# Gates of the first token tile: one-hot products on TensorE, or adding scatters issued from GpSimd

## The chip, the cores and the metric

The kernel runs on one core of one Trainium2 chip. TensorE multiplies, VectorE (DVE), ScalarE (ACT) and GpSimd (POOL) work on tiles in on-chip memory, SyncE (SP) issues most DMAs, and 16 DMA engines move the data. Every engine works through a queue of its own in order, and the queues wait for each other by semaphores. The metric is the device time in microseconds of one execution, as the median of several runs; a profile is one further execution of its own.

## The reference, cut to what matters

Two transformer blocks run over 512 tokens of width 1024. The first (convolution and sliding attention, then a feed forward of width 2816) and the attention of the second are not touched, apart from DMAs set beside the feed forward. The change is in the last layer of the second block, which picks 128 of 16384 experts for every token, 16 in each of 8 heads:

```python
def peer(xn, wq, subkeys, u_tab, v_tab):
    q = (xn @ wq).reshape(bsz, s, PEER_HEADS, 2, PEER_HALF)
    sub = jnp.einsum('bshpd,hpnd->bshpn', q, subkeys, preferred_element_type=jnp.float32)
    s_top, i_top = lax.top_k(sub, PEER_TOPK)
    cand = (s_top[..., 0, :, None] + s_top[..., 1, None, :]).reshape(...)
    cand_idx = (i_top[..., 0, :, None] * N_KEYS + i_top[..., 1, None, :]).reshape(...)
    best, pos = lax.top_k(cand, PEER_TOPK)
    expert = jnp.take_along_axis(cand_idx, pos, axis=-1)
    gate = jax.nn.softmax(best, axis=-1)
    ...
        a = jax.nn.gelu(jnp.einsum('td,ted->te', xb, ub, preferred_element_type=jnp.float32))
        return jnp.einsum('te,ted->td', (gb * a).astype(vb.dtype), vb)
```

## The kernel before

The 512 tokens are four tiles of 128. Three of them (TD = 384 tokens) go **dense**: all 16384 experts are computed for them, 128 at a time (a "unit" x of 128 experts, NEXP = 128 units), and weighted by a gate matrix that is zero where an expert was not chosen. The fourth tile goes **by rows**: GpSimd gathers the chosen rows of the two tables, 128 rows each, one table row for each token per gather.

Dense, up: for unit x TensorE makes a 128 x 384 product in 24 matmuls (8 chunks, each in three products of high and low parts: L449, L452, L453). ScalarE applies the gelu (L1538) and SP stores it to DRAM (`activations`, L1027).

Dense, gates: for each token the gate matrix is a 128 x 128 matrix, the sum over its 128 choices of a one-hot column times a one-hot row times the gate. VectorE makes the one-hots of four tokens (a "four") in two instructions (L2268, L2272, tile `hots`), TensorE multiplies them (four matmuls, L930; the trace has two records for each), ScalarE copies the result into `Gs` (L1567). After 16 fours (64 tokens) ScalarE issues a 4 MB DMA of `Gs` into the DRAM tensor `gate_matrices` (gd, L1572). It holds TSTAY = 256 tokens; the last 128 of the 384 stay in `Gs`. `fours_of(x)` says which fours follow the product of unit x: the 96 fours lie behind the 64 units from FIRST_GATE_UP = 43 on, one and two in turn. The lists of choices are turned by TensorE first (L922, tile `sel`).

Dense, down: for each unit VectorE multiplies activation and gate (`weigh`, L2301, L2302) and TensorE adds 18 products into six banks. SP fetches activation and gate rows back (`load_weighing`, L1035, L1036), the first NAG = 4 units together at unit LOAD_AT = 124 of the up stage.

Rows: GpSimd issues 256 gathers (L1118, rows of `y`, four buffers, so gather r waits until row r - 4 is used). VectorE uses each: for the first 128 a row product (L2247), for the others a multiply-add into hN (L2255). `rows_until` sets how many rows stand in VectorE's queue before each unit: one per unit in the 64 units with gates, eight in five units after them.

Weights: unit by unit through three buffers `wraw`; SP loads (L987), ScalarE rounds to the high part `WH` (L1139), VectorE subtracts to get the low part `WL` (L2236; GpSimd does so before the expert stage, L1110). What sets the order is the order of the written loops on each engine. In the up stage VectorE's loop is, for unit x: one-hots of unit x + 1, the rows of unit x, `WL` of unit x + 2.

## Time and profile before

| | |
|---|---|
| median of 3 runs | 2197.84 us (2195.1 to 2200.02) |
| the profiled execution | 2191.74 us, of it a span of 2190.0 us |
| TensorE busy | 2142.9 us, 98% of the span |
| VectorE, ScalarE, GpSimd busy | 1477.7, 886.4 and 856.1 us |
| feed forward, weights issued | 214 to 572 us |
| up stage with gates | first hots product 1218.8 us, last 1566.6 us |

The span is what lies between the first and the last instruction; the profile's times are counted from its start. "Busy" is the time under instructions. The idle time before an instruction is given with the event that ended it. A wait of an engine matters if the engine that ends last stands behind it.

### The profile page before, as it was taken

The page shows a single profiled execution, that of the slowest core. Times are in us where ns is not written, and L with a number is a line of the kernel's source. Part 1 is how long each engine was busy: PE and PEld are TensorE (multiplying, and loading weights), DVE is VectorE, ACT ScalarE, POOL GpSimd, SP SyncE. Part 2 cuts the span into 40 slices and gives each one's busy share as a digit, 9 for nine tenths or more (in the row PEclk, how much of TensorE's full clock was granted, in tenths as well). Part 3 has the DMA queues.
Part 4 walks back from the last instruction along what each step waited for, and adds up shares of the span by engine and source line. Part 5 has one row for each costly group of instructions (what it writes and reads, how often), then busy time and mean ns, then how long its engine had stood idle before and what let it go on. Part 6 is the DMA issues. An engine that isn't in the chain of part 4 may idle for free.

```text
span 2190.0 us, 29584 instructions
## 1 busy us (share of the span) xinstructions
PE 2142.9 (98%) x10879; PEld 1864.9 (85%) x10879; DVE 1477.7 (67%) x2763; ACT 886.4 (40%) x1341; POOL 856.1 (39%) x450
## 2 busy tenths in 40 slices
PE   7989999999999999999999999999998999999999
PEld 6757888888877877899999999999997888888887
DVE  5973411110146994346879999999767999999887
ACT  5355422232253444343334555555433333333332
POOL 1003244444333433345667422222343455434452
PEclk9999999999999999999999999999999999999999
DMA  5302233333342322344444899997799999999996
GB/s 176 97 7 65 93 97 97 97 98 87 92 121 68 88 67 86 97 138 135 132 136 147 269 307 295 302 290 260 255 358 333 374 372 380 376 374 365 375 351 256
DMA packets 222219, 444.10 MB, mean 203 GB/s; under 512 B 83803, under 2 KB 133884, under 8 KB 221948
## 3 DMA queue, kind: packets, MB, share of 16 engines
q1 hardware_dynamic: 119612, 291.20, 39.5%
q0 software_dynamic: 36864, 134.23, 17.2%
q10 hardware_dynamic: 65600, 16.78, 3.4%
q8 instruction: 87, 1.43, 0.3%
q14 instruction: 56, 0.46, 0.1%
HBM read 397.71 MB, written 44.43 MB: 202 GB/s over the span
## 4 chain that ended last, share of the span: by engine, by line
PE 87%; DVE 7%; ACT 2%; DMA 2%; issue 1%; POOL 1%; SPq 0%; DVEq 0%; ACTq 0%; POOLq 0%
PE bank L449 26%; PE bank L452 26%; PE bank L453 26%; PE bank L930 4%; DVE cacc L1734 1%; DMA wraw<-in_peer_u 1%; DVE m L1927 1%; PE bank L899 1%; POOL WL L1110 1%; DVE xn L1928 1%; PE bank L621 1%; ACT sc L1250 1%; ACT WH L1139 0%; PE bank L836 0%; DMA wraw<-in_w_in 0%
## 5 line engine op out<-in xcount | busy, mean ns | idle before, releaser
L1110 POOL TENSOR_TENSOR WL<-wraw,WH 128x1024 fp32r<-128x1024 f32 x182 | 467.7, 2575 | 736.7 <-ACT WH L1139 736.7
L1139 ACT ACTIVATE WH<-wraw 128x1024 fp32r<-128x1024 f32 x411 | 435.2, 1060 | 619.1 <-PE bank L449 341.0
L449 PE MATMUL bank<-XH,WH 128*128 128x384 f32 (+2 forms) x1864 | 668.4, 359 | 12.3 <-DVE WL L2236 5.2
L452 PE MATMUL bank<-XL,WH 128*128 128x384 f32 (+2 forms) x1864 | 657.9, 353 | 0.0
L453 PE MATMUL bank<-XH,WL 128*128 128x384 f32 (+2 forms) x1864 | 657.9, 353 | 0.0
L449 PEld LDWEIGHTS bank<-XH,WH 128*128 128x128 f32 x1864 | 352.0, 189 | 44.2 <-issue 11.2
L452 PEld LDWEIGHTS bank<-XL,WH 128*128 128x128 f32 x1864 | 352.0, 189 | 28.5 <-issue 0.7
L453 PEld LDWEIGHTS bank<-XH,WL 128*128 128x128 f32 x1864 | 351.4, 189 | 28.5
L2236 DVE TENSOR_TENSOR WL<-wraw,WH 128x1024 fp32r<-128x1024 f32 x229 | 279.6, 1222 | 105.5 <-ACT WH L1139 98.9
L1118 POOL DMA_INDIRECT y<-in_peer_u_rows,gidx x128 | 182.1, 1423 | 356.8 <-DVE gdot L2247 346.3
L449 PE MATMUL bank<-WH,GH 128*128 128x512 f32 x768 | 299.2, 390 | 1.9 <-issue 1.6
L453 PE MATMUL bank<-WH,GL 128*128 128x512 f32 x768 | 298.9, 389 | 0.0
L452 PE MATMUL bank<-WL,GH 128*128 128x512 f32 x768 | 298.8, 389 | 0.0
L1118 POOL DMA_INDIRECT y<-in_peer_v,gidx x128 | 204.2, 1595 | 209.2 <-DVE hN L2255 188.1
L449 PEld LDWEIGHTS bank<-WH,GH 128*128 128x128 f32 x768 | 144.2, 188 | 33.4 <-issue 3.5
L453 PEld LDWEIGHTS bank<-WH,GL 128*128 128x128 f32 x768 | 144.2, 188 | 29.9
L452 PEld LDWEIGHTS bank<-WL,GH 128*128 128x128 f32 x768 | 144.2, 188 | 29.7
L2255 DVE SCALAR_TENSOR_TENSOR hN<-y,gdot,hN 128x1024 f32<-128x1024 f32 x128 | 163.7, 1279 | 2.9
L1538 ACT ACTIVATE ac<-bank 128x384 f32<-128x384 f32 x122 | 59.7, 490 | 241.7 <-PE bank L453 237.3
L1852 DVE TENSOR_TENSOR y<-bank,y 128x512 f32<-128x512 f32 x22 | 15.2, 691 | 208.2 <-PE bank L453 208.2
L2247 DVE CUSTOM_DVE_ANT_0 y<-y,x_nat 128x1024 f32<-128x1024 f32 x128 | 154.8, 1219 | 1.2 <-DMA y<-in_peer_u_rows,gidx 1.1
L2268 DVE TENSOR_TENSOR hots<-iota,sq 128x1024 f32<-128x1024 f32 x96 | 117.1, 1219 | 2.7 <-ACT rt L1549 2.7
(304 smaller groups left out, 2577.9 us busy)
## 6 DMA issues: line engine op xcount, KB each, us to landing
wraw<-in_peer_u SPq DMA_DIRECT2D x128, 512.0 KB
wraw<-in_peer_v SPq DMA_DIRECT2D x128, 512.0 KB
activations<-ac SPq DMA_DIRECT2D x122, 192.0 KB
ar<-activations SPq DMA_DIRECT2D x122, 192.0 KB
gate_matrices<-Gs ACTq DMA_DIRECT2D x4, 4096.0 KB, 35.7
gr<-gate_matrices SPq DMA_DIRECT2D x128, 128.0 KB
wraw<-in_w_gate SPq DMA_DIRECT2D x22, 512.0 KB
wraw<-in_w_up SPq DMA_DIRECT2D x22, 512.0 KB
```

The costliest lines, as they stand in the source:

```text
L449: mm = pe.matmul(out, wh, xh, start=first, stop=False)
L452: pe.matmul(out, wh, xl, start=False, stop=False)
L453: return pe.matmul(out, wl, xh, start=False, stop=last)
L930: mm = pe.matmul(out[:, r * P:(r + 1) * P], hots[:, q, 1, r, :], hots[:, q, 0, r, :], start=True, stop=True)
L1110: pool.tensor_tensor(WL[:, u % NW, 0:m], wraw[:, u % NR, 0:m], WH[:, u % NW, 0:m].bitcast(F32), ALU.subtract).then_inc(s("w_lo"), 1)
L1118: pool.indirect_dma_start(out=gathered[:, row % NGATHER, :], out_offset=None, in_=(u_rows if row < HS else v_rows)[:, :], in_offset=bass.I ...
L1139: act.activation(WH[:, u % NW, 0:k * n], wraw[:, u % NR, 0:k * n], ACT.Copy).then_inc(s("w_hi"), 1)
L1538: act.activation(ac[:, x % NAC, :] if x < SENT else kept[:, x - SENT, :], src[:, 0:TD], ACT.Gelu_apprx_tanh).then_inc(frees(("a", x)), 1)
L2236: dve.tensor_tensor(WL[:, u % NW, 0:k * n], wraw[:, u % NR, 0:k * n], WH[:, u % NW, 0:k * n].bitcast(F32), ALU.subtract).then_inc(made, 1)
L2247: dve.tensor_tensor_reduce(out=at, in0=at, in1=x_nat[:, :], scale=1.0, scalar=0.0, op0=ALU.mult, op1=ALU.add, accum_out=gdot[:, row:row + ...
L2255: dve.scalar_tensor_tensor(out=hN[:, NTD, :], in0=at, scalar=gdot[:, row - HS:row - HS + 1], in1=hN[:, NTD, :], op0=ALU.mult, op1=ALU.add) ...
L2268: link(dve.tensor_tensor(hots[:, q, :, :, :], iota128[:, :].unsqueeze(1).unsqueeze(1).to_broadcast([P, 2, TOK4, P]), ijcol[:, :, tok].unsq ...
```

## The change

The first of the three dense tiles no longer has its gates formed by TensorE. `fours_of` now deals out 64 fours over the same 64 units, one each, and the sel tile of the first token tile isn't turned. In place of that:

- SP writes zeros over the first tile's part of `gate_matrices`, in 16 DMAs of 512 KB (runs of 256 B), one after every fourth weight load from feed forward unit ("wg", 4) on.
- VectorE makes, behind `gidx`, the addresses of the first tile's gates: (expert number) x 256 + token (three instructions: `scat_expert`, `scat_gate`, `scat_at`).
- GpSimd issues 128 indirect DMAs that add: number k adds, for each of the 128 tokens, its gate k to its cell in DRAM. Two follow each of the first 64 gathers. Before every sixteenth it waits until all earlier ones have landed, since two heads may have chosen the same expert.
- Of the 4 MB stores of `Gs` the first two fall away.
- SP loads the first gates and activations back from unit 120 on, one pair every second unit, and waits at unit 120 for all scatters.

```diff
...
+TSCAT = P
+FIRST_FOUR = TSCAT // TOK4
...
+SCAT_PER_ROW = 2
+ZRUN = 64
+ZBLOCKS = 8
-LOAD_AT = NEXP - 4
+LOAD_AT = NEXP - 2 * NAG
...
-    return range(b * NFOUR // GATE_UPS, (b + 1) * NFOUR // GATE_UPS)
+    fours = NFOUR - FIRST_FOUR
+    return range(FIRST_FOUR + b * fours // GATE_UPS, FIRST_FOUR + (b + 1) * fours // GATE_UPS)
...
+        with ExitStack() as under:
+            scat_at = sb("scat_at", [P, HS], U32, under)
+            scat_gate = sb("scat_gate", [P, HS], F32, under)
+            scat_expert = sb("scat_expert", [P, HS], F32, under)
...
+        own_row = sb("own_row", [P, 1], F32)
...
+            zeros = sb("zeros", [P, ZRUN], F32, sc)
...
+        gate_cells = gd.rearrange("x p (t a) -> (x p t) a", a=1)
...
                     if x == FIRST_GATE_UP - UP_AFTER_SEL:
-                        for t in range(NTD):
+                        for t in range(TSCAT // P, NTD):
...
                     tile(("u", x), ("a", x), tokens=TD)
                     for four in fours_of(x):
                         out = take("gm", four)
-                        pe.wait_ge(s("hots_made"), four + 1)
+                        pe.wait_ge(s("hots_made"), four - FIRST_FOUR + 1)
                         q = four % NQ
...
+                if u >= unit_at[("wg", 4)] and (u - unit_at[("wg", 4)]) % 4 == 0 and u < unit_at[("wg", 4)] + 4 * (NEXP // ZBLOCKS):
+                    if u == unit_at[("wg", 4)]:
+                        sp.wait_ge(s("zeros_made"), 1)
+                    half, x = (u - unit_at[("wg", 4)]) // 4 % 2, (u - unit_at[("wg", 4)]) // 8 * 2 * ZBLOCKS
+                    sp.dma_start(gd[x:x + 2 * ZBLOCKS, :, half * ZRUN:(half + 1) * ZRUN].rearrange("x p t -> p x t"),
+                                 zeros[:, :].unsqueeze(1).to_broadcast([P, 2 * ZBLOCKS, ZRUN])).then_inc(
+                                     s("zeroed"), 16)
...
                         if x == LOAD_AT:
                                 wait_full(sp, ("gm", four))
-                            for tt in range(NGT - NGSTAY):
+                            sp.wait_ge(s("scattered"), 16 * HS)
+                            for tt in range(TSCAT // GTOK, NGT - NGSTAY):
                                 sp.wait_ge(s(f"g_out{tt}"), 16)
-                            for n in range(NAG):
-                                load_weighing(n)
+                        if x >= LOAD_AT and (x - LOAD_AT) % 2 == 0:
+                            load_weighing((x - LOAD_AT) // 2)
...
+            pool.iota(own_row[:, :], pattern=[[1, 1]], base=0, channel_multiplier=1,
+                      allow_small_or_imprecise_dtypes=True).then_inc(s("own_row_made"), 1)
+            pool.memset(zeros[:, :], 0.0).then_inc(s("zeros_made"), 1)
...
+            def scatter(k):
+
+                if k == 0:
+                    pool.wait_ge(s("scatter_made"), 1)
+                    pool.wait_ge(s("zeroed"), 16 * (NEXP // ZBLOCKS))
+                elif k % SEL == 0:
+                    pool.wait_ge(s("scattered"), 16 * k)
+                pool.indirect_dma_start(out=gate_cells[:, :],
+                                        out_offset=bass.IndirectOffsetOnAxis(ap=scat_at[:, k:k + 1], axis=0),
+                                        in_=scat_gate[:, k:k + 1], in_offset=None, compute_op=ALU.add).then_inc(
+                                            s("scattered"), 16)
+
             for row in range(2 * HS):
...
                                         in_offset=bass.IndirectOffsetOnAxis(ap=gidx[:, row % HS:row % HS + 1], axis=0)
+                for k in range(min(row * SCAT_PER_ROW, HS), min((row + 1) * SCAT_PER_ROW, HS)):
+                    scatter(k)
...
                     if x == FIRST_GATE_UP - UP_AFTER_SEL:
-                        for t in range(NTD):
+                        for t in range(TSCAT // P, NTD):
...
             def copy_gates(four):
                 tt, at = four // per, four % per * TOK4
-                if at == 0 and tt >= 2:
+                if at == 0 and tt >= TSCAT // GTOK + 2:
...
+                expert = step(dve.scalar_tensor_tensor(out=scat_expert[:, :], in0=sel[:, 0, 0, :], scalar=float(N_KEYS),
+                                                       in1=sel[:, 1, 0, :], op0=ALU.mult, op1=ALU.add))
+                dve.tensor_copy(scat_gate[:, :], sel[:, 2, 0, :])
+                dve.wait_ge(s("own_row_made"), 1)
+                dve.wait_ge(s("dve_link"), expert)
+                dve.scalar_tensor_tensor(out=scat_at[:, :], in0=scat_expert[:, :], scalar=float(TSTAY),
+                                         in1=own_row[:, 0:1].to_broadcast([P, HS]), op0=ALU.mult, op1=ALU.add).then_inc(
+                                             s("scatter_made"), 1)
...
                     for four in fours_of(x):
-                        if four >= NQ:
+                        if four >= FIRST_FOUR + NQ:
...
-                for t in range(NTD):
+                for t in range(TSCAT // P, NTD):
```

GpSimd's queue, from the end of the weight work on. Before:

```order
L1110 TENSOR_TENSOR WL<-wraw,WH 128x1024 [waits w_begun,w_hi] x100
L1118 DMA y<-in_peer_u_rows,gidx 128x1024 [waits index_made]
```

After (scat_gate holds the gates, scat_at the addresses):

```order
L1134 TENSOR_TENSOR WL<-wraw,WH 128x1024 [waits w_begun,w_hi] x100
L1154 DMA y<-in_peer_u_rows,gidx 128x1024 [waits index_made]
L1145 DMA gate_matrices<-scat_gate,scat_at 4194304x1 [waits zeroed,scatter_made]
L1145 DMA gate_matrices<-scat_gate,scat_at 4194304x1
L1154 DMA y<-in_peer_u_rows,gidx 128x1024
L1145 DMA gate_matrices<-scat_gate,scat_at 4194304x1 x2
```

Gathers 1, 2 and 3, which followed each other directly, now stand behind two, four and six scatters.

VectorE's queue at the beginning of the stage, from the end of the choice of experts. Before:

```order
L2225 SCALAR_TENSOR_TENSOR gidx<-sel 128x128
L2228 COPY ggate<-sel 128x128
L2236 TENSOR_TENSOR WL<-wraw,WH 128x1024
L2268 TENSOR_TENSOR hots<-iota,sq 128x1024
L2272 TENSOR_TENSOR hots<-hots,rt 128x512
L2236 TENSOR_TENSOR WL<-wraw,WH 128x1024
L2247 ISA y,gdot<-y,x_nat 128x1024
L2247 ISA gdot 128x1
L2247 ISA y,gdot<-y,x_nat 128x1024
L2247 ISA gdot 128x1
L2268 TENSOR_TENSOR hots<-iota,sq 128x1024
L2272 TENSOR_TENSOR hots<-hots,rt 128x512
```

After:

```order
L2263 SCALAR_TENSOR_TENSOR gidx<-sel 128x128
L2266 COPY ggate<-sel 128x128
L2267 SCALAR_TENSOR_TENSOR scat_expert<-sel 128x128
L2269 COPY scat_gate<-sel 128x128
L2272 SCALAR_TENSOR_TENSOR scat_at<-scat_expert,own_row 128x128
L2282 TENSOR_TENSOR WL<-wraw,WH 128x1024
L2314 TENSOR_TENSOR hots<-iota,sq 128x1024
L2318 TENSOR_TENSOR hots<-hots,rt 128x512
L2282 TENSOR_TENSOR WL<-wraw,WH 128x1024
L2293 ISA y,gdot<-y,x_nat 128x1024
```

Three instructions are added ahead of the WL of the next unit; where two pairs of hots stood (every second unit), one pair stands.

SP's queue where the first gates are loaded back. Before:

```order
L1027 DMA activations<-ac 128x384
L1035 DMA ar<-activations 128x384
L1036 DMA gr<-gate_matrices 128x256
L1035 DMA ar<-activations 128x384
L1036 DMA gr<-gate_matrices 128x256
L1035 DMA ar<-activations 128x384
L1036 DMA gr<-gate_matrices 128x256
L1035 DMA ar<-activations 128x384
L1036 DMA gr<-gate_matrices 128x256
L987 DMA wraw<-in_peer_u 128x1024 x3
```

After:

```order
L1040 DMA activations<-ac 128x384
L1048 DMA ar<-activations 128x384
L1049 DMA gr<-gate_matrices 128x256
L1000 DMA wraw<-in_peer_u 128x1024
L1040 DMA activations<-ac 128x384
L1000 DMA wraw<-in_peer_u 128x1024
L1040 DMA activations<-ac 128x384
L1048 DMA ar<-activations 128x384
L1049 DMA gr<-gate_matrices 128x256
L1000 DMA wraw<-in_peer_u 128x1024
```

Eight loads that stood together are four pairs, with two weight loads between one pair and the next.

## Rows read from the trace of the kernel before

**Rows 1.** The page: span, busy times, the DMA engines in 40 slices (tenths busy).

```profile
span 2190.0 us, 29584 instructions
...
PE 2142.9 (98%) x10879; PEld 1864.9 (85%) x10879; DVE 1477.7 (67%) x2763; ACT 886.4 (40%) x1341; POOL 856.1 (39%) x450
...
DMA  5302233333342322344444899997799999999996
```

**Rows 2.** Waits of TensorE, whole span: us in total, times, longest.

```profile
PE bank L498 <- DVE y L1635: 11.6, 3, 9.0
...
PE bank L449 <- DVE WL L2236: 5.2, 1, 5.2
```

**Rows 3.** Windows: length, busy us (count) by engine, clock, DMA share, GB/s.

```profile
1205.00:1310.00 105.00, 105.00 (x682) 104.97 (x682) 98.34 (x118) 55.27 (x73) 37.74 (x24) 1.00 0.88 285
1310.00:1415.00 105.00, 105.00 (x690) 105.00 (x690) 98.03 (x118) 58.46 (x68) 26.60 (x19) 1.00 0.93 295
1415.00:1570.00 155.00, 155.00 (x1016) 155.00 (x1015) 137.67 (x166) 82.59 (x98) 40.60 (x29) 1.00 0.84 269
1570.00:1660.00 90.00, 84.84 (x479) 84.33 (x478) 60.95 (x85) 29.57 (x40) 45.32 (x32) 0.96 0.94 337
```

**Rows 4.** Timeline of TensorE: start, duration, count; transposes of sel, then gate products.

```profile
1209.51 1.14 PE L922 MATMUL bank<-ident,sel 128*128 128x128 f32 x9
...
1542.89 1.95 PE L930 MATMUL bank<-hots 128*128 128x128 f32 x16
1544.60 0.42 PE L449 MATMUL bank<-XH,WH 128*128 128x384 f32 x1
...
1548.84 1.05 PE L930 MATMUL bank<-hots 128*128 128x128 f32 x8
1549.65 0.42 PE L449 MATMUL bank<-XH,WH 128*128 128x384 f32 x1
```

**Rows 5.** A group of 1205 to 1570 us: count, busy us, mean ns, idle before, releasers.

```profile
L1118 POOL DMA_INDIRECT y<-in_peer_u_rows,gidx x71 | 102.4, 1442 | 256.5 <-DVE gdot L2247 255.0 <-issue 0.9 <-DVE gidx L2225 0.7
```

**Rows 6.** Timeline of POOL: start, duration, in brackets the idle time before.

```profile
1210.44 0.94 POOL L1118 DMA_INDIRECT y<-in_peer_u_rows,gidx  x1 [0.31 <-issue]
...
1212.93 0.97 POOL L1118 DMA_INDIRECT y<-in_peer_u_rows,gidx  x1 [0.30 <-issue]
...
1300.68 1.68 POOL L1118 DMA_INDIRECT y<-in_peer_u_rows,gidx  x1 [2.46 <-DVE gdot L2247]
```

**Rows 7.** Timeline of VectorE at the same places.

```profile
1207.61 0.29 DVE L2225 SCALAR_TENSOR_TENSOR gidx<-sel 128x128 uint32<-128x128 f32 x1
1207.96 1.22 DVE L2236 TENSOR_TENSOR WL<-wraw,WH 128x1024 fp32r<-128x1024 f32 x1
1211.86 1.23 DVE L2268 TENSOR_TENSOR hots<-iota,sq 128x1024 f32<-128x1024 f32 x1 [2.68 <-ACT rt L1549]
1216.89 1.23 DVE L2247 CUSTOM_DVE_ANT_0 y<-y,x_nat 128x1024 f32<-128x1024 f32 x1 [0.81 <-DMA y<-in_peer_u_rows,gidx]
...
1300.33 1.22 DVE L2236 TENSOR_TENSOR WL<-wraw,WH 128x1024 fp32r<-128x1024 f32 x1
1301.46 1.22 DVE L2268 TENSOR_TENSOR hots<-iota,sq 128x1024 f32<-128x1024 f32 x1
1302.72 0.69 DVE L2272 TENSOR_TENSOR hots<-hots,rt 128x512 f32<-128x512 f32 x1
```

**Rows 8.** DMA queues: packets, MB, share of 16 engines' span.

```profile
q0 software_dynamic: 36864, 134.23, 17.2%
q10 hardware_dynamic: 65600, 16.78, 3.4%
```

**Rows 9.** Around the eight loads: SP, ScalarE, TensorE in time.

```profile
1632.30 0.30 SPq L1035 DMA_DIRECT2D ar<-activations  x1
...
1644.63 1.06 ACT L1139 ACTIVATE WH<-wraw 128x1024 fp32r<-128x1024 f32 x1 [8.33 <-DMA wraw<-in_peer_u]
...
1647.09 0.66 PE L449 MATMUL bank<-XH,WH 128*128 128x384 f32 x1 [5.16 <-DVE WL L2236]
```

## The prediction

> **What bounds the kernel now.** The page first: TensorE is busy 98% of a 2190.0 us span, and the granted clock is full in the stretches that matter here, 1.00 [rows 1, 3]. The waits of TensorE, whole span: one of 9.0 us, one of 5.2 us [rows 2], and none of the others above 3.4. So time comes off only if TensorE gets less work or loses a wait, and comes on as soon as another engine's queue falls behind. The windows over the stretch in which the gates are made then show how near the others are [rows 3]: VectorE is busy 98 of 105 us, the DMA engines 0.88 and 0.93, POOL (GpSimd) 38 and 27 of 105. From 1570 to 1660 us the DMA share is 0.94 and TensorE is short by 5.2 us. The change acts on this stretch.
>
> **Part 1, TensorE's gate products (removed: a third).** After each expert's 24 products come one or two "fours". In the timeline a unit followed by two fours has its 16 records from 1542.89 and goes on at 1544.60, 1.71 us; with one four from 1548.84 to 1549.65, 0.81 us [rows 4]. Before: 96 fours in 64 units, so 32 units with two and 32 with one: 32 x 1.71 + 32 x 0.81 = 80.6 us. After: 64 fours, one per unit: 64 x 0.81 = 51.8 us. Gain 28.8 us, all on the path, since TensorE waited for nothing there. Three of the nine transposes of sel go too, nine took 1.14 us [rows 4]: 0.4 us. A whole unit with one four runs from 1544.60 to 1549.65, 5.05 us; one with two is 0.90 longer, so the mean was 5.50 and the 64 units take 323 instead of 352 us.
>
> **Part 2, VectorE and ScalarE.** Each dropped four takes 1.22 + 0.69 us from VectorE [rows 7] and one copy from ScalarE, which is busy half of the stretch [rows 3]. VectorE per unit: one four 1.91, one row product 1.23, one WL 1.22 = 4.36 of 5.05 us [rows 7], 86% where the windows have 89 to 94% [rows 3]. It gains air. Three small instructions are added behind gidx, at about 0.3 us each (gidx took 0.29 [rows 7]), 0.8 us before the WL that the next unit needs; that WL started at 1207.96 us [rows 7] and its unit at 1214.6 (the first hots product starts at 1218.8 us, less one expert product of 1544.60 to 1548.84 = 4.2 us [rows 4]), so they cost nothing.
>
> **Part 3, POOL: the term that decides.** POOL issued one gather per unit and gets two scatters to each of the first 64. No scatter is in this trace; the nearest row is the gather's issue, also DMA_INDIRECT with 128 indices. Its time is not constant. With VectorE idle at its start it takes 0.94 us, and issues follow each other at 0.30 us of "issue" [rows 6]: 1.25 us each. The one at 1300.68 took 1.68: it began while VectorE ran WL from 1300.33 to 1301.55, and 1300.68 + 1.68 = 1302.36 is 0.81 after that instruction's end, though VectorE went straight on with another [rows 6, 7]. The one at 1212.93 began under the first hots instruction (1211.86 to 1213.09) and ended 0.81 after its end as well [rows 6, 7]. So an issue waits for the VectorE instruction that is running at its start, then needs 0.81 us of its own; the next starts 0.81 + 0.30 = 1.11 us behind a VectorE boundary, just as an instruction of 1.22 us ends that began at the boundary (WL at 1300.33, the next at 1301.46: 1.13 us apart [rows 7]). If the scatter costs what the gather does, POOL gets one issue per long VectorE instruction, and the 0.69 us one lets it slip: three issues per unit. Three are wanted. The Trainium skill has this as a rule ("SBUF — State Buffer", section "Who interferes with whom": a VectorE instruction with two SBUF inputs and a GpSimd one that reads SBUF exclude each other for the whole instruction); the trace agrees, by the 0.81 us.
> The same from the sums: from 1205 to 1570 us POOL's 71 issues took 102.4 us at 1.44 mean, and it was idle 256.5 us [rows 5]. 64 rows' share of that is 231 us, less the 29 us saved: 202 us. 128 scatters need 128 x 1.25 = 160 us at best, 128 x (1.44 + 0.30) = 223 at the mean, 128 x 1.98 = 254 if each met a running instruction. I take the low end, since back-to-back issues start near a boundary.
> Queued behind POOL: the gathers, and behind those VectorE's row product, which stands ahead of WL in VectorE's order, and behind WL TensorE. The cover is the lead of four rows: a gather may go out 4 units (20 us) ahead and lands about 6.4 us after its issue (second gather at 1210.44, VectorE waited for it until 1216.89 [rows 6, 7]), so 13 us of lateness are hidden. At the start there is no lead: gather 1 now goes out after two scatters, near 1213, and VectorE waits some 2.5 us longer; TensorE sees about 1 us, as the WL behind the next row product is wanted two units after 1214.6, at 1224.7. Every 16 scatters POOL waits until all earlier ones have landed. They lie in one queue behind a gather with 6.4 us to land: 2 to 3 us, 7 times, 14 to 21 us against the 13 us of cover: 1 to 8 us, I take 2. Part 3 in all: +3 us, bounds +1 and +9 while the scatter's issue costs the gather's.
>
> **Part 4, DMA.** 16.78 MB of gate stores took 3.4% of 16 engines' span, 74 us, for 65600 packets of 256 B: 18 ns each [rows 8]. Half goes: -37 us of DMA time in the stretch. The zeroing is the same 37 us (32768 packets), but beside the feed forward, which runs from 214 to about 580 us, slices 5 to 11, 0.2 to 0.4 busy [rows 1]: 16 DMAs of 2.3 us each, a weight load then lands at most 2.3 us later and is prefetched three units ahead; nothing. The scatters add 128 x 128 = 16384 element packets; at 18 ns 18 us, at a 4 KB packet's time (17.2% of 16 x 2190 us over 36864 packets = 163 ns [rows 8]) 167 us. I take the low end, for the size. DMA time of the stretch was 0.88 x 105 + 0.93 x 105 + 0.84 x 155 = 320 us of 365 [rows 3]; it becomes 320 - 37 + 18 = 301 of 336: 0.90, as before, no cost.
>
> **Part 5, the loads of gates and activations, spread.** SP issued eight loads in a row from 1632.30 us, 1.25 MB, ahead of a weight load. ScalarE then waited 8.33 us for that weight load and TensorE 5.16 us [rows 9]; the granted clock of the window is 0.96 [rows 3]. 21 units lie between the last hots product (1566.6 + 0.8) and the first product of the down stage (1663.1, behind 1.6 us of issue), 94 us; at 0.173 us a product they need 21 x 4.16 = 87.4: 6.6 us lost. Now a pair of loads goes out every second unit from unit 120. SP waits there for the scatters too, but their last is issued near unit 105. The bytes stay, at a share of 0.94, so not all comes back: -4 us, bounds 0 and -6.6.
>
> **Sum.** -28.8 - 0.4 + 3 + 0 - 4 = -30 us. The profiled run has 2191.7 us (span 2190.0), the median of the runs 2197.8, 6 us above. Forecast on the median: 2168 us. Its own bounds: -29.2 + 1 - 6.6 = -35, and -29.2 + 9 + 0 = -20, with some more if the clock dips: 2160 to 2185.
>
> **Rivals.**
> A, slower: POOL becomes the pace. If the scatter's own time is not 0.81 but 1.2 to 1.6 us (one and a half times to twice the gather's, which no row excludes), the next issue comes 1.5 to 1.9 us behind a VectorE boundary, in the middle of the second instruction, and waits for that one's end near 2.3. A scatter then costs two VectorE instructions, a unit 2 x 2.3 + 1.1 = 5.7 us at least, 6.0 with the waits for landings. 64 units: 365 to 384 us against 352 before: +13 to +32, less 4 of part 5: 2207 to 2226 us, and up to 2240 if the landings add more. It decides from about 0.2 us more per scatter. For it: the 202 us of room against 223 at the mean. Against: same instruction, same 128 indices. The Trainium skill ("Collectives: The Full Stack", section "Stop ④ — SDMA + CCE: where bytes move and the add happens") describes an add in the DMA engine as two reads and one write; no row here shows an adding DMA, and by that rule alone this rival would be the forecast if POOL's 0.81 us went mostly into read descriptors.
> B, no change, or a small gain: scatters a little dearer (0.1 to 0.2 us), POOL falls behind in some units; units of 5.2 to 5.5 us. 64 x 0.15 to 0.45 = 10 to 29 us given back, more with the waits: 2185 to 2206 us.
> C, the element packets are slow. 16384 at 52 ns (53 us) fill the 336 us; at 80 ns the stretch is as long as before; at 163 ns it needs 283 + 167 = 450 us, +85: up to 2280 us. Long landings would do the same through the seven waits. The stretch is already near 0.9, which speaks for it.
> D, the change does less than it says: POOL ends its scatters later than unit 120 and SP blocks the weights. It would take a pace of 6 us or more, and belongs to A and C.
>
> **How the numbers follow.** Forecast 45%. B 14%, A 26%, C (and worse) 15%. Range for 8 in 10: 2160 to 2245, leaving out 3% below and most of C above. About 0.2% (4.4 us) is what a measurement of this kernel can tell from no change: faster by more than that holds the forecast and half of B: 52%. Within it: 6%. Slower: the rest of B, A, C: 42%.
>
> **What would show it.** Part 1: 512 records of hots products instead of 768, a unit of 5.05 us. Part 3 right: scatter issues of 0.94 to 1.7 us, VectorE's waits for gathered rows small, TensorE's waits for WL small between 1215 and 1540 us. Wrong (A): scatter issues above 1.2 us with VectorE idle, POOL busy or at "issue" without a break over the first 64 rows, VectorE waiting for y at most rows, TensorE for WL. C: DMA share at 1.0, POOL waiting for its own scatters, ScalarE for wraw. Part 4: TensorE's waits in the feed forward unchanged. Part 5: the 5.16 us wait gone, clock 1.0 there. The forecast fails as a whole if the gathers land late.

## Result and profile after

The changed kernel takes 2239.82 us (median of 6 runs, 2233.04 to 2240.76) against 2198.93 us for the kernel before on the same chip (6 runs): a ratio of 1.0188, 95% interval 1.0173 to 1.0202. It is **slower by 41 us**, where the forecast was 30 us faster. The profiled execution has a span of 2239.2 us, 49.2 more than before's.

Where the 49 us lie, by the landmarks of the two traces:

| | before | after | difference |
|---|---|---|---|
| first hots product starts | 1218.8 | 1226.6 | +7.8 |
| first to last hots product | 347.8 | 386.5 | **+38.7** |
| last hots product to first product of the down stage | 96.5 | 96.7 | +0.2 |
| down stage and end | 526.9 | 529.4 | +2.5 |

So nearly all of it is in the stretch from the first to the last hots product, called the stage below, where TensorE has a third less of gate products to do. Lines of the page that answer to [rows 1] (busy us, share of the span, instructions; then the DMA engines in 40 slices):

```profile
span 2239.2 us, 29066 instructions
...
PE 2144.1 (96%) x10620; PEld 1854.1 (83%) x10620; DVE 1427.0 (64%) x2702; ACT 857.6 (38%) x1306; POOL 1111.2 (50%) x580
...
DMA  4302344444332223344445788977899999999996
```

TensorE is busy as long as before with 259 instructions fewer, VectorE is busy 51 us less, and GpSimd 255 us more. The windows of the stage of after (as in [rows 3]):

```profile
1205.00:1310.00 105.00, 91.35 (x526) 89.90 (x525) 74.44 (x86) 41.17 (x55) 83.44 (x49) 0.93 0.71 195
1310.00:1415.00 105.00, 91.78 (x552) 90.33 (x552) 71.81 (x86) 43.75 (x52) 88.10 (x52) 0.97 0.90 246
1415.00:1570.00 155.00, 137.35 (x805) 135.90 (x805) 106.03 (x126) 62.64 (x75) 131.33 (x78) 0.93 0.86 230
```

In the first two windows GpSimd (the fifth busy figure of a line) went from 38 and 27 to 83 and 88 of 105 us, VectorE fell from 98 to 74 and 72, and TensorE from 105 to 91 and 92. The clock fell from 1.00 to 0.93 to 0.97. The DMA share went from 0.88, 0.93 and 0.84 to 0.71, 0.90 and 0.86, while the bytes moved fell from 285, 295 and 269 to 195, 246 and 230 GB/s. GpSimd's two groups of DMA issues in the up stage (count, busy us, mean ns, idle time before them by what ended it); [rows 5] has the gathers of before:

```profile
L1145 POOL DMA_INDIRECT gate_matrices<-scat_gate,scat_at x128 | 240.6, 1879 | 40.9 <-issue 37.7 <-DMA gate_matrices<-scat_gate,scat_at 3.3
L1154 POOL DMA_INDIRECT y<-in_peer_u_rows,gidx x128 | 178.2, 1392 | 123.5 <-DVE gdot L2293 92.6 <-issue 24.1 <-DVE gidx L2263 6.8
```

Who waits for whom follows from VectorE's and TensorE's waits over the whole span (us in total, times, longest); before, TensorE had one wait for `WL` [rows 2] and VectorE's waits for gathered rows came to 1.1 us:

```profile
DVE y L2293 <- DMA y<-in_peer_u_rows,gidx: 125.9, 61, 6.6
```

```profile
PE bank L462 <- DVE WL L2282: 50.5, 34, 5.2
```

An ordinary row of the stage, first as the chain of what ended last between 1397 and 1412 us (start, us, what):

```profile
1397.07 1.55 POOL gate_matrices L1145
1398.62 0.30 issue
1398.93 1.15 POOL y L1154
1400.07 0.30 issue
1400.38 2.55 POOL gate_matrices L1145
1402.92 0.30 issue
1403.23 1.55 POOL gate_matrices L1145
1404.78 0.30 issue
1405.09 1.07 POOL y L1154
```

and VectorE's timeline in the same row (start, duration, in brackets the idle time before):

```profile
1400.25 1.22 DVE L2314 TENSOR_TENSOR hots<-iota,sq 128x1024 f32<-128x1024 f32 x1
1401.50 0.69 DVE L2318 TENSOR_TENSOR hots<-hots,rt 128x512 f32<-128x512 f32 x1
1404.06 1.23 DVE L2293 CUSTOM_DVE_ANT_0 y<-y,x_nat 128x1024 f32<-128x1024 f32 x1 [1.86 <-DMA y<-in_peer_u_rows,gidx]
```

GpSimd goes through gather, scatter, scatter without a break but the 0.30 us of issue: from 1398.93 to 1405.09, 6.16 us a row. A unit of TensorE with one four needs 5.05. The scatter at 1403.23 began with VectorE idle and took 1.55 us. The one at 1400.38 began under the hots instruction that ended at 1401.47 and itself ended 1.46 us after that. It is the pattern that the prediction read from the gathers, with 1.46 us where it put 0.81. GpSimd's first gather began at 1216.49 and its 65th at 1606.52: 64 rows in 390 us, 6.09 us a row. The stage, which is 63 units and a little more, has 386.5 us, 6.12 us a unit.

### The profile page after: what moved, and what is told of

The parts are those of the page before. It is cut to its first block, busy times and chain, and to the rows that moved or that the text cites. A ratio compares the mean times of both kernels' runs of the same rounds, so it can differ in the third digit from the quotient of the medians.

```text
span 2239.2 us, 29066 instructions
## 1 busy us (share of the span) xinstructions
PE 2144.1 (96%) x10620; PEld 1854.1 (83%) x10620; DVE 1427.0 (64%) x2702; ACT 857.6 (38%) x1306; POOL 1111.2 (50%) x580
## 3 DMA queue, kind: packets, MB, share of 16 engines
q0 software_dynamic: 55296, 134.31, 18.9%
## 4 chain that ended last, share of the span: by engine, by line
PE 68%; POOL 13%; DVE 6%; DMA 6%; issue 4%; ACT 2%; SPq 0%; DVEq 0%; ACTq 0%; POOLq 0%
PE bank L462 21%; PE bank L465 21%; PE bank L466 21%; POOL gate_matrices L1145 9%; POOL y L1154 3%; DMA wraw<-in_peer_u 2%; DMA y<-in_peer_u_rows,gidx 2%; DVE m L1965 1%; DMA wraw<-in_peer_v 1%; PE bank L912 1%; DVE xn L1966 1%; PE bank L634 1%; DMA gate_matrices<-scat_gate,scat_at 0%; ACT WH L1177 0%; PE bank L511 0%
## 5 line engine op out<-in xcount | busy, mean ns | idle before, releaser
L1134 POOL TENSOR_TENSOR WL<-wraw,WH 128x1024 fp32r<-128x1024 f32 x182 | 476.7, 2625 | 729.7 <-ACT WH L1177 729.7
L462 PE MATMUL bank<-XH,WH 128*128 128x384 f32 (+2 forms) x1864 | 676.5, 363 | 56.7 <-DVE WL L2282 50.5
L466 PE MATMUL bank<-XH,WL 128*128 128x384 f32 (+2 forms) x1864 | 664.8, 357 | 0.0
L462 PEld LDWEIGHTS bank<-XH,WH 128*128 128x128 f32 x1864 | 357.4, 192 | 95.1 <-issue 62.6
L465 PEld LDWEIGHTS bank<-XL,WH 128*128 128x128 f32 x1864 | 357.8, 192 | 28.6 <-issue 0.7
L466 PEld LDWEIGHTS bank<-XH,WL 128*128 128x128 f32 x1864 | 356.5, 191 | 28.6
L1154 POOL DMA_INDIRECT y<-in_peer_v,gidx x128 | 213.4, 1667 | 201.3 <-DVE hN L2301 177.0
L1145 POOL DMA_INDIRECT gate_matrices<-scat_gate,scat_at x128 | 240.6, 1879 | 40.9 <-issue 37.7
```

The lines of the kernel that those rows point to most:

```text
L462: mm = pe.matmul(out, wh, xh, start=first, stop=False)
L465: pe.matmul(out, wh, xl, start=False, stop=False)
L466: return pe.matmul(out, wl, xh, start=False, stop=last)
L1134: pool.tensor_tensor(WL[:, u % NW, 0:m], wraw[:, u % NR, 0:m], WH[:, u % NW, 0:m].bitcast(F32), ALU.subtract).then_inc(s("w_lo"), 1)
L1145: pool.indirect_dma_start(out=gate_cells[:, :], out_offset=bass.IndirectOffsetOnAxis(ap=scat_at[:, k:k + 1], axis=0), in_=scat_gate[:, k:k ...
L1154: pool.indirect_dma_start(out=gathered[:, row % NGATHER, :], out_offset=None, in_=(u_rows if row < HS else v_rows)[:, :], in_offset=bass.I ...
```

## The experiments

The question is what makes GpSimd's row so long, and whether it alone costs the time. **Theory A**: the issue of an accumulating scatter (one that adds) is dearer than a gather's, GpSimd becomes the pace of a row, VectorE waits for gathered rows and TensorE for VectorE. Against it stand rival C (the element packets, or their landings), a price for each scatter wherever it stands, and a share for the zeroing and the later start.

**One scatter in place of 128** (all else as changed; in each run with fewer scatters the number that SP waits for at unit 120 follows, which the diffs don't show):

```diff
-                for k in range(min(row * SCAT_PER_ROW, HS), min((row + 1) * SCAT_PER_ROW, HS)):
+                for k in range(row, row + 1) if row < 1 else ():
```

> The changed kernel with one scatter instead of 128: the gates of the first token tile are then left out of the matrix, apart from one pick's. Zeroing, TensorE's two tiles, the spread loads and all 256 gathers stay. Theory A (GpSimd's issue of the scatters, 240.6 us of its time, is what VectorE and then TensorE wait for): VectorE's waits for gathered rows fall from 125.9 us to under 10, TensorE's 34 waits of 50.5 us for the hot rows go, its clock stays whole in the stage, and the stage of the gate products comes to about 318 us (347.8 less the 28.8 of half the products, and little more); the whole at 2165 to 2180 us. Rival C (the accumulating packets hold the DMA queues up) expects the same time here, so this run alone doesn't part the two; its DMA waits would say so. Rival: the later start (the transposes 6.4 us later) and the zeroing cost something of their own, then it stays at 2185 or above.

Measured: 2166.74 us, ratio 0.9861 (0.9837 to 0.9885). First to last hots product: 1222.8 to 1542.3 us, 319.5 us. The window over that stretch:

```profile
1222.60:1542.40 319.80, 319.80 (x2028) 319.80 (x2026) 266.12 (x320) 159.12 (x190) 72.04 (x66) 1.00 0.86 281
```

TensorE is busy in all of it, at full clock. Without its scatters the change thus comes out where it was forecast (2168 us), and the 73 us between this run and the change come with the other 127 scatters. VectorE's instructions aren't slowed by them: some 320 took 266 us here and 317 took 265 in the change (the line stands under **The clock** below). VectorE waits.

**64 scatters, one a row:**

```diff
-                for k in range(min(row * SCAT_PER_ROW, HS), min((row + 1) * SCAT_PER_ROW, HS)):
+                for k in range(row, row + 1) if row < HS // 2 else ():
```

> The changed kernel with 64 scatters instead of 128, one beside each of the first 64 gathers; the other half of the first tile's gates is left out. Theory A: GpSimd has in each of these rows one gather of 1.39 and one scatter of 1.88 us, 3.3 us in place of 6.1, against a row of VectorE and TensorE of about 4.5 us (318 us over some 71 rows), so it is not the pace of the row any more; the stage stays near 325 us and the whole at 2170 to 2190 us, nearly all of the loss gone with half the scatters. A cost that were in proportion to the scatters (each at its own price on the path, or each packet's in the DMA queues) would leave half of the loss: about halfway between the run with one scatter and the change, 2200 to 2210 us.

Measured: 2171.81 us, ratio 0.9883 (0.9862 to 0.9905). The stage is 319.6 us, as with one scatter, though each scatter takes GpSimd as long as in the change:

```profile
L1145 POOL DMA_INDIRECT gate_matrices<-scat_gate,scat_at x64 | 120.4, 1882 | 25.4 <-issue 18.9 <-DMA gate_matrices<-scat_gate,scat_at 6.5
```

Half of the scatters cost 5 us of the 73. The two profiles are 7.6 us apart, and 5.3 of these are there already at `gidx` (1217.4 and 1212.1), ahead of the first scatter. A cost in proportion is out.

**96 scatters**, one and two a row by turns (`range(row * 3 // 2, (row + 1) * 3 // 2)` over 64 rows in place of the same loop):

> The changed kernel with 96 accumulating scatters, one and two by turns beside each of the first 64 gathers; a quarter of the first tile's gates is left out. The runs so far: one scatter 2166.7 us, 64 scatters 2171.8, 128 scatters 2239.8. Theory A with a point from which GpSimd decides: the stage of 319.5 us without loss has 64 rows, 4.99 us a row; with 1.5 scatters a row GpSimd needs about 1.39 + 1.5 x 1.88 + 2.5 x 0.3 = 4.96 us, just at the row, and VectorE is up to four rows behind before it waits. So little is lost: 2172 to 2190 us. If each scatter beyond the 64th costs its share, it is the middle, 2206 us; if the loss is the number of GpSimd's issues in a row of two (a burst that closes the buffer of four rows), nearly half of it as well.

Measured: 2184.08 us, ratio 0.9942 (0.9924 to 0.9960). The curve over 1, 64, 96 and 128 scatters is 2166.7, 2171.8, 2184.1, 2239.8 us: flat, a bend, then 1.7 us for each scatter.

**64 scatters crowded into 32 rows**, the same number at twice the rate:

```diff
-                for k in range(min(row * SCAT_PER_ROW, HS), min((row + 1) * SCAT_PER_ROW, HS)):
+                for k in range(2 * row, 2 * row + 2) if row < HS // 4 else ():
```

> The changed kernel with 64 accumulating scatters, as in the run that took 2171.8 us, but two beside each of the first 32 gathers in place of one beside each of the first 64; half of the first tile's gates is left out. Theory A, the pace of a row: in 32 rows GpSimd needs 6.1 us a row against TensorE's and VectorE's 4.99, 32 x 1.1 = 35 us less the four rows of the buffer (some 6 us), and half-clock stretches of some 5 to 10 us beside it; then it keeps pace. 2197 to 2212 us. Rival, the number of accumulating scatters (their packets, or GpSimd's time beside VectorE, wherever they stand): 2172 us again, within 3.

Measured: 2205.69 us, ratio 1.0032 (1.0020 to 1.0045): 34 us above the run with the same number of scatters one a row. It is their rate that costs, not their number. Two windows (columns as in [rows 3]), the first over the crowded rows:

```profile
1229.00:1410.00 181.00, 159.80 (x955) 157.86 (x954) 125.02 (x150) 75.57 (x90) 151.18 (x91) 0.95 0.86 232
1410.00:1586.00 176.00, 172.80 (x1077) 172.64 (x1076) 143.91 (x173) 82.81 (x100) 42.71 (x40) 0.98 0.87 275
```

TensorE is short by 21 us where GpSimd is busy 151 of 181 us, and by 3 us where it is not.

**Plain writes in place of adding ones**, all 128 at the same places:

```diff
-                                        in_=scat_gate[:, k:k + 1], in_offset=None, compute_op=ALU.add).then_inc(
+                                        in_=scat_gate[:, k:k + 1], in_offset=None).then_inc(
```

> The changed kernel with the accumulation taken out of the scatters: each is a plain write of its 128 gates, same addresses, same 128 issues; where two picks of a token fall on one expert the later one stands alone. Theory A with the cost in the issue of any scattered store: GpSimd's 1.55 us unblocked and 1.88 us mean stay, and the time stays within 3 us of 2240. Rival: the accumulation is what makes the issue longer than the gather's (1.55 against 0.94 us unblocked): then an issue falls to about 0.94, the row of GpSimd to some 4.5 us, and the time to 2190 to 2215 us. By rival C the packets' time falls (no read of the old value), and with it the time, while the issue does not.

Measured: 2193.23 us, ratio 0.9975 (0.9960 to 0.9990). The scatter's line (ns, shortest, median, longest) and its group:

```profile
L1145 POOL DMA_INDIRECT gate_matrices<-scat_gate,scat_at x128: 972/1308/2002, 1217.7 to 1557.9; - x128
```

```profile
L1145 POOL DMA_INDIRECT gate_matrices<-scat_gate,scat_at x128 | 184.1, 1438 | 53.1 <-issue 36.9 <-DMA gate_matrices<-scat_gate,scat_at 16.2
```

With VectorE idle a plain one takes 0.97 us, the adding one 1.55, the gather 0.94. So asking for the add puts 0.58 us on GpSimd's issue, and without it 46.6 us of the loss are gone. The rival that the run was made for holds, and theory A in its narrow form (any scattered store is that dear) does not. The edit changes the packets too: the software queue of this run has 40960, that of the change 55296 and that of before 36864 [rows 8]. The next run halves the packets at the same number of issues.

**Scatters of 64 partitions**, still 128 of them: half of the addresses and packets.

```diff
-                                        out_offset=bass.IndirectOffsetOnAxis(ap=scat_at[:, k:k + 1], axis=0),
-                                        in_=scat_gate[:, k:k + 1], in_offset=None, compute_op=ALU.add).then_inc(
+                                        out_offset=bass.IndirectOffsetOnAxis(ap=scat_at[0:P // 2, k:k + 1], axis=0),
+                                        in_=scat_gate[0:P // 2, k:k + 1], in_offset=None, compute_op=ALU.add).then_inc(
```

> The changed kernel with all 128 accumulating scatters, but each of 64 partitions in place of 128: half the packets and half the addresses at the same number of issues; the gates of tokens 64 to 127 are left out. If an issue costs by its count of addresses, unblocked it falls from 1.55 to about 0.8 to 1.0 us, GpSimd's row from 6.1 to about 4.9 us, and the time to 2175 to 2200 us. If it costs a fixed amount for each issue, it stays at 1.55 and the time at 2235 to 2245 us, although the DMA queues have half the scatter packets: that would also close the case against the packets (rival C).

Measured: 2232.49 us, ratio 1.0153 (1.0132 to 1.0175), 7 us below the change, and a little below the range that was expected of a fixed price.

```profile
L1145 POOL DMA_INDIRECT gate_matrices<-scat_gate,scat_at x128: 1417/1500/2469, 1218.3 to 1595.2; - x128
```

Half the addresses take 0.14 us off an issue of 1.55: most of it is a fixed price. And half of the scatters' addresses and packets took 7 us off, no more than the shorter issues explain (128 x 0.09 us of mean, 11.7 us). Rival C is closed for this kernel: had the packets been the bound, about half of the 73 us would have gone.

**Part 4 alone**, the zeroing DMAs in the kernel before:

```diff
+                if u >= unit_at[("wg", 4)] and (u - unit_at[("wg", 4)]) % 4 == 0 and u < unit_at[("wg", 4)] + 4 * (NEXP // ZBLOCKS):
...
+                    sp.dma_start(gd[x:x + 2 * ZBLOCKS, :, half * ZRUN:(half + 1) * ZRUN].rearrange("x p t -> p x t"),
+                                 zeros[:, :].unsqueeze(1).to_broadcast([P, 2 * ZBLOCKS, ZRUN])).then_inc(
+                                     s("zeroed"), 16)
```

> The kernel before with part 4 alone: the sixteen zeroing DMAs beside the feed forward, the rest as before. The change's gate stage began 7.8 us later than before's, the one-scatter run's 3.8, the others' 5 to 9. If the zeroing did it: 2200 to 2205 us, with the first peer_u weights landing some 3 us later. If that start only drifts from run to run (the one-scatter and 64-scatter programs are the same up to there and differ by 5 us): within 1.5 us of 2196.7.

Measured: 2195.48 us, ratio 0.9993 (0.9983 to 1.0002). The zeroing costs nothing that can be told from noise. The first hots product starts at 1222.7 us, 3.9 later than in the profile of before. The next run has no zeroing and starts it at 1221.9, so the zeroing isn't what moves this start.

**Part 5 alone**, the spread loads in the kernel before:

```diff
-LOAD_AT = NEXP - 4
+LOAD_AT = NEXP - 2 * NAG
...
-                            for n in range(NAG):
-                                load_weighing(n)
+                        if x >= LOAD_AT and (x - LOAD_AT) % 2 == 0:
+                            load_weighing((x - LOAD_AT) // 2)
```

> The kernel before with part 5 of the change alone: the waits for the written gates and the first pair of loads stand at the first of the last eight gate units, and a pair of loads follows at every second unit, in place of all eight together four units before the end. The prediction gave it 4 us (0 to 6.6): 2191 to 2198 us. The change's own trace showed 96.7 us from the last hot product to the first down product against 96.5 before: by that it is worth nothing there, within 1 us of 2197.8; and where the loads wait for the fourth tile half's gates earlier, SP could hold back weight loads: up to 2205 us.

Measured: 2193.82 us, ratio 0.9987 (0.9975 to 0.9999), 2.9 us faster, which is only just clear of nothing. TensorE's waits from 1570 to 1665 us:

```profile
PE bank L449 <- DVE WL L2236: 2.2, 1, 2.2
PE bank L449 <- issue: 1.6, 1, 1.6
```

The wait of 5.16 us [rows 9] is 2.2, and from the last hots product to the down stage it is 93.5 us instead of 96.5.

**A version of what was learned: 64 tokens scattered, one scatter a row.** The second 64 partitions carry the same tokens' other eight picks of a head, so 64 scatters hold all gates of 64 tokens. Only these 64 tokens' part is zeroed (8 DMAs), and GpSimd waits for landings before every eighth scatter. TensorE makes 80 fours.

```diff
-TSCAT = P
+TSCAT = P // 2
...
+                        act.wait_ge(s("scatter_made"), 1)
+                        for table in (scat_at, scat_gate):
+                            by_head = table.rearrange("p (h s) -> p h s", h=PH)
+                            act.dma_start(by_head[P // 2:P, :, 0:SEL // 2],
+                                          by_head[0:P // 2, :, SEL // 2:SEL]).then_inc(s("halves_moved"), 16)
...
-                for k in range(min(row * SCAT_PER_ROW, HS), min((row + 1) * SCAT_PER_ROW, HS)):
+                for k in range(row - 2, row - 1) if 2 <= row < 2 + HS // 2 else ():
```

> A whole kernel: 64 tokens in place of 128 are scattered, with 64 accumulating scatters in place of 128. The first 64 partitions carry eight of the sixteen picks of a head, and the other 64 the same tokens' other eight, brought there by two small DMAs; only the first half tile is zeroed, TensorE forms the gates of the other 320 (80 fours instead of 64 in the change and 96 before). One scatter stands beside each of gathers 2 to 65. Theory A: GpSimd keeps pace as in the run with 64 scatters (2171.8 us), TensorE has 16 fours more of 0.90 us, 14.4 us, so 2183 to 2190 us: 7 to 14 us below before and some 50 below the change. Rival: the gain of half the change is lost to something that comes with any accumulating scatter (its time on GpSimd beside VectorE, or the clock): 2195 us or above.

Measured: 2184.20 us, ratio **0.9943** (0.9927 to 0.9959): faster than the kernel before by 12 to 14 us and than the change by 56. The stage, 333.9 us, is the 319.6 of the runs without loss and 16 fours of 0.90 us, 14.4:

```profile
1224.80:1558.90 334.10, 334.10 (x2155) 334.10 (x2153) 293.16 (x350) 173.45 (x206) 210.15 (x131) 1.00 0.94 280
```

TensorE has no wait and full clock in it, with 64 accumulating scatters of 1.87 us beside it and a DMA share of 0.94. GpSimd waited 23.5 us for landings of its own scatters here, which cost nothing, since it wasn't the pace.

## Why the prediction was wrong

Its point was 2168 us and its forecast faster; it is 2239.8, near the top of the range. It is **rival A** in its mechanism, GpSimd as the pace, and in its place. Its unit of 5.7 to 6.0 us was a little short (measured 6.12), its 2207 to 2226 us lacked some 14, and its "up to 2240" held. The detail differs: rival A lets each scatter wait for two VectorE instructions, but in the change 53 of the 128 began with no VectorE instruction running, because VectorE itself was waiting for its row. Point by point:

**Parts 1 and 2, right.** Gate products: forecast -28.8 us; the run with one scatter has a stage of 319.5 us in place of 347.8, 28.3 less. VectorE did gain the air, and spent it waiting.

**Part 3, the step that failed**: "I take the low end, since back-to-back issues start near a boundary", which also needs its condition "If the scatter costs what the gather does". The whole part was put at +3 us, bounds +1 and +9, and the runs show +67. Two choices in it were wrong, and the runs price each.
- The price of the adding scatter: 1.55 us and not 0.94 with VectorE idle, 1.45 and not 0.81 behind a VectorE instruction. The range of the rival was 1.2 to 1.6, and it "decides from about 0.2 us more". The plain writes show what this choice cost: 46.6 us.
- The low end at the gather's price. The plain writes do cost what the gather does (0.97), and still their stage is 342.8 us, 23 above the 319.5, where the text allowed +9. They took 1.44 us in the mean, as the gathers of [rows 5] did, not 0.95: 84 of the 128 began under a running VectorE instruction.

The prediction's own room, 202 us that GpSimd has free beside 64 gathers, and its cover, 13 us of lateness that the lead of four rows hides, were good. A check made afterwards, in us: the time for which the scatters hold GpSimd's queue (busy and idle before, from the groups of each run), less this room and this cover, against the time that the stage grew.

| run | scatters hold GpSimd | less 202 and 13 | stage over 319.5 |
|---|---|---|---|
| 64, one a row | 145.8 | none | 0.1 |
| plain, 128 | 237.2 | 22 | 23 |
| 96 | 235.6 | 21 | 16 |
| 64 partitions, 128 | 270.8 | 56 | 58 |
| the change | 281.5 | 67 | 67 |

In the crowded run the scatters hold GpSimd for 139.0 us in half the rows, so against 101 and 13 us: 25, measured 36.7. There the formula is 12 us short, of which the time after the crowded rows is a part (below). With 96 scatters it is 5 us too high.

So "223 at the mean" against 202 already said that the cover would be used up, and 128 x (1.88 + 0.30) = 279 us would have given the rest.

**The clock**, of which the text had only "with some more if the clock dips", lies inside this loss and not on top of it. TensorE's 2027 or 2028 products of the stage were busy 319.8 us with one scatter; in the change they are

```profile
1226.30:1613.30 387.00, 342.00 (x2027) 337.09 (x2025) 265.02 (x317) 159.81 (x190) 325.81 (x191) 0.95 0.84 228
```

22.2 us longer, at a mean clock of 0.95. With the 45 us of waits that is the 67 us. But GpSimd's 6.1 us a row account for all 67, and by this reckoning a TensorE at full clock would have waited longer instead. The clock went to its half level (1.2 of 2.4 GHz) at seven of the nine waits of 2 us or more in the stage, within the wait or up to 1.6 us behind it. Two windows around one of them, a wait of 4.91 us that ended at 1337.30:

```profile
1330.00:1336.00 6.00, 2.40 (x17) 2.20 (x15) 1.22 (x3) 1.51 (x2) 5.04 (x4) 1.00 1.06 300
1336.00:1342.70 6.70, 5.40 (x17) 5.43 (x18) 6.63 (x10) 1.06 (x1) 5.83 (x3) 0.50 1.20 338
```

In the crowded run a part comes on top, since there the pace of GpSimd ends halfway: the second window has 3 us of waiting, and its clock of 0.98 is worth some 3.5 us more (0.02 of 176, an estimate). No run held the clock and kept the stalls, so this share is read, not tested.

**The landings**: the prediction put the seven waits at 14 to 21 us, 1 to 8 of them behind the cover, and took 2. They came to 3.3 us in the change (in its group above) and to 16.2 with plain writes, whose issues are shorter. The size is right for the plain writes and too high for the change; the term decided nothing.

**Part 4, right in the time, wrong in one size.** The zeroing cost nothing (2195.48 against 2197.85 us), and the stores of `Gs` fell from 3.4% to 1.8% of the span, 34 us less where 37 were forecast. But the element packets were put at 18 us of DMA time, "the low end, for the size". The queue's lines, of the change and of the plain writes (packets, MB, share of 16 engines' span):

```profile
q0 software_dynamic: 55296, 134.31, 18.9%
```

```profile
q0 software_dynamic: 40960, 134.31, 17.2%
```

Against the 17.2% of 2190 us before [rows 8], 377 us, the adding scatters took 423, some 46 us more; the plain writes stayed at 377. This cost no time in the change, where the DMA share of the stage is 0.84. It would matter if GpSimd were quicker: the stage without loss has a share of 0.86 of 319.8 us, 275, and 275 + 46 = 321 fill it (an estimate). So by this estimate adding scatters issued at the gather's price would have found hardly any DMA time free. No run shows that case.

**Part 5, right alone, lost in the change**: forecast -4, alone -2.9 us and with one scatter 93.5 us from the last hots product to the down stage. In the change this is 96.7 us: the wait of 5.16 us is gone, but three smaller ones (4.4 us together) stand there. Why was not tried. Over the nine profiled kernels with spread loads the stretch takes 91.3 to 99.0 us, over the two without them 96.5 and 97.9, so a single profile says little about 3 us.

**The sum**, with the measured terms: -28.3 + 67 + 0.2 is +38.9, the measured +38.7 and +0.2. What is left of the profile's 49 us is +7.8 before the first hots product and +2.5 behind, and the change causes neither as far as the profiles show. The start differs by 7 us between programs that are the same up to it (1222.8 with one scatter, 1229.5 with the crowded 64), and the medians, 41 us apart, hold less of it. VectorE's choice of experts, from its first instruction (`stop`) to `gidx`, took 254.9 us in the profile of before and 260.0 to 260.3 in all ten others, also in the kernel that differs only in the spread loads. These are the two groups that grew, in the change:

```profile
L2208 DVE TENSOR_TENSOR hot<-hot,itf 128x2048 f32<-128x2048 f32 x8 | 22.5, 2813 | 0.0
L2199 DVE TENSOR_TENSOR hot<-bhf,iota 128x2048 f32<-128x2048 f32 x8 | 20.5, 2567 | 0.3
```

They had 18.2 and 18.3 us before. The last two, 4.49 and 4.38 us in place of 2.29, lie in the change over GpSimd's `WL` instructions at 1202.88 and 1205.63. So some 5 us of the +7.8 belong to how these two engines met in the one profile of before, and the rest lies ahead of the choice of experts, which began at 950.1 to 958.8 us in the eleven profiles. The last part, from the down stage on, takes 526.4 to 530.0 us in all of them, which covers the +2.5.

**Rivals B, C, D.** B's 2185 to 2206 us is where the plain writes came out. C is closed by the 64-partition run and by GpSimd, which waited 3.3 us in all for its scatters. D did not occur.

## What to carry to other kernels

A queue that has a third of its time free is not free for an operation that no row prices: work out from which price it becomes the pace, and if that is 0.2 us off the guess, issue it at half the rate first. What such an issue costs GpSimd is mostly a fixed price for each DMA (1.42 us with 64 indices, 1.55 with 128), so fill all partitions and issue fewer; what it costs the kernel depends on its rate against the row: next to nothing up to a point (64 scatters in 64 rows), and most of its 2.2 us of issue behind it (1.7 us for each from the 97th on). Where a sum has a low end and a mean, and nothing measured speaks for the low end, the mean is the forecast.

## What the hardware showed

- An indirect DMA with 128 indices held GpSimd 0.94 us as a gather, 0.97 us as a plain scatter and 1.55 us as an adding one, VectorE being idle; with 64 indices the adding one took 1.42 us.
- An issue that starts under a VectorE instruction waits for its end, and then takes 0.81 us (gather, in the kernel before), 0.86 (plain scatter) or 1.45 us (adding scatter), medians of 88, 84 and 75 issues. The Trainium skill ("SBUF — State Buffer", section "Who interferes with whom") has the exclusion for instructions of GpSimd that read SBUF; these runs show it for the issue of an indirect DMA too. The section also tells of a probe in which `tensor_tensor` did not stall a DMA; here the tensor-tensor instruction held the scatter's issue at 1400.38 until 1401.47.
- The adding scatters' packets cost DMA time, but no more than the engines had free: the queue took some 46 us more of 16 engines than before, the plain scatters none, and the share was 0.71 to 0.90 in the change, against 0.84 to 0.93 before [rows 3]. The Trainium skill ("Collectives: The Full Stack", section "Stop ④ — SDMA + CCE: where bytes move and the add happens") describes an add as two reads and one write; the adding scatters' greater DMA time fits that, though no run counts the reads. What made the kernel slower was GpSimd's issue.
